# Attention with negated scores, first keys over two queues, and constants loaded as rows and turned by TensorE

## What is computed

```python
h = _norm(x) * (1 + scale1) + shift1           # shift, scale from silu(c) @ w_ada + b_ada
za, zb, q, k, v = split(h @ w_in)              # 512 | 256 | 512 | 512 | 512 columns
# A: gelu(za) -> u, v; v normed, mixed over 128 positions by a_ws, + a_bs; u * v
# B: 2-D DFT of zb, times f_w
# C, latent queries: 8 heads x 64, window of 8 x 16 keys + 512 cached context keys
s_loc = where(mask, q @ k.T * scale + rpb, -inf); s_ctx = q @ kc.T * scale
p = softmax(concat([s_loc, s_ctx]));              o = p_loc @ v + p_ctx @ vc
y = concat([A, B, C]) @ w_out; x = LN(alpha * x + gate1 * y); then a gated ConvFFN
```

## Time and profile before

| | |
|---|---|
| median of 3 runs | 2999.77 us (2996.41 to 3000.17) |
| the profiled execution, its own time | 3001.65 us |
| its span | 2999.9 us |
| PE busy | 2750.9 us (92%) |
| DVE, ACT, POOL busy | 1789.2, 1239.6, 472.0 us |
| mean granted clock of PE | 0.961 |

### The profile page before, as it was taken

One profiled execution on the slowest core, in us unless ns is written; L12 is line 12 of the kernel. 1 busy time (PEld: TensorE's weight loads), 2 busy tenths in 40 slices (PEclk: granted clock), 3 DMA queues, 4 the chain that ended last, 5 costly groups with the idle time before them and its releaser, 6 DMA issues. The chain is left out here.

```text
span 2999.9 us, 49988 instructions
## 1 busy us (share of the span) xinstructions
PE 2750.9 (92%) x17010; PEld 2484.5 (83%) x17010; DVE 1789.2 (60%) x3028; ACT 1239.6 (41%) x2612; POOL 472.0 (16%) x678
## 2 busy tenths in 40 slices
PE   4899999766999996997899999999999979999996
PEld 3899999655777785886899999999999968888875
DVE  3533432155999893776887876667666634452545
ACT  2111111124888882233655565556555522111121
POOL 0000000043444331224000000100000000320312
PEclk8999999878999997998899999999999989999998
DMA  8223222398576543563655564444444344344234
GB/s 277 85 74 123 85 85 71 136 372 170 118 148 141 114 91 98 186 209 117 189 166 171 177 200 160 152 151 147 154 150 153 124 158 150 99 133 140 77 126 133
DMA packets 405309, 435.71 MB, mean 145 GB/s; under 512 B 127228, under 2 KB 298254, under 8 KB 402448
## 3 DMA queue, kind: packets, MB, share of 16 engines
q1 hardware_dynamic: 379664, 415.20, 46.3%
q10 hardware_dynamic: 23168, 10.38, 1.2%
q0 software_dynamic: 2304, 7.88, 0.7%
HBM read 311.18 MB, written 124.57 MB: 145 GB/s over the span
## 5 line engine op out<-in xcount | busy, mean ns | idle before, releaser
L2138 PE MATMUL fu_alpha<-fu_h,fu_w 128*128 128x384 f32 x3168 | 576.1, 336 | 17.7 <-DVE fu_h L2364 10.6
L2624 PE MATMUL fd_acc<-fd_w,fd_f 128*128 128x512 f32 x2376 | 546.8, 392 | 27.2 <-DVE fd_w L2652 17.6
L2138 PEld LDWEIGHTS fu_alpha<-fu_h,fu_w 128*128 128x128 f32 x3168 | 554.9, 189 | 20.3 <-issue 20.2
L2624 PEld LDWEIGHTS fd_acc<-fd_w,fd_f 128*128 128x128 f32 x2376 | 447.5, 189 | 126.5 <-issue 18.3
L2138 PE MATMUL fu_beta<-fu_h,fu_w 128*128 128x384 f32 x1584 | 287.2, 336 | 0.6 <-DVE fu_h L2364 0.6
L2138 PEld LDWEIGHTS fu_beta<-fu_h,fu_w 128*128 128x128 f32 x1584 | 277.1, 189 | 1.1 <-issue 1.1
L579 PE MATMUL pj_gps<-pj_ht,w_in 128*128 128x256 f32 x2160 | 270.4, 286 | 0.0
L579 PEld LDWEIGHTS pj_gps<-pj_ht,w_in 128*128 128x128 f32 x2160 | 265.1, 192 | 1.3
L2648 DVE TENSOR_TENSOR fd_f<-fd_f_stage,fd_f 128x512 fp32r<-128x512 f32 (+1 forms) x110 | 91.3, 832 | 285.1 <-ACT fd_f L2604 285.1
L2604 ACT CAST fd_f<-fd_f_stage 128x512 fp32r<-128x512 f32 (+1 forms) x110 | 63.4, 579 | 444.1 <-PE fd_acc L2624 403.1
L2338 DVE TENSOR_TENSOR fu_w<-up_w_stage,fu_w 128x512 fp32r<-128x512 f32 x264 | 181.7, 689 | 85.7 <-ACT fu_w L2202 82.7
(11 more groups left out here) (218 smaller groups left out, 4161.6 us busy)
## 6 DMA issues: line engine op xcount, KB each, us to landing
up_w_stage<-in_w_gu_dram SPq DMA_DIRECT2D x88, 512.0 KB, 4.2
fu_w_sums<-w_gu_sums SPq DMA_DIRECT2D x132, 256.0 KB, 3.2
fd_w_stage<-in_w_down_dram SPq DMA_DIRECT2D x54, 512.0 KB, 3.7
fd_f_stage<-f_t SPq DMA_DIRECT2D x88, 256.0 KB, 2.7
at_k<-k_t SPq DMA_DIRECT2D x28, 704.0 KB, 12.5
w_gu_sums<-fu_w_sums SPq DMA_DIRECT2D x66, 256.0 KB, 4.5
fo_w<-in_w_ada_dram SPq DMA_DIRECT2D x8, 2048.0 KB, 14.8
up_w_stage<-in_w_gu_dram SPq DMA_DIRECT2D x44, 256.0 KB, 4.5
```

The lines of the kernel that those rows point to most:

```text
L2138: mm = pe.matmul(out, w[x][:, j, k, :], b[y][:, j, k, :], start=opens and (k, x, y) == (0, HI, HI), stop=(k, x, y) == (KH - 1, LO, HI), sk ...
L2624: mm = pe.matmul(acc[:, t, at], f[a][:, slot, t * P:(t + 1) * P], w[b][:, w_at(st, slot), at], start=is_step(st, 0) and (a, b) == (HI, HI) ...
```

## The change

The conditioning vectors, `b_ada` and `a_bs` arrive as 36 rows of 128 elements in an unused half of `zbt`; PE turns them in one transpose ahead of everything, ACT takes SiLU and DVE copies the rest from PSUM. `f_w` is issued after SiLU. In group 0 the rounding of weight blocks 4 to 8 is spread between the products on ACT and DVE, and `norm_x(2)` moves behind them (POOL follows). In attention `q` is stored with the factor negated, masks are +1e30, the bias is mask - rel, so that DVE seeks minima: the context minimum is the start value of the reduction over the window, which gives the bias of the exponentials (scale -1) itself. L1452 goes; a one-element copy that waits for the first reduction comes in. The sum of partial outputs is written at the head of the step instead of its end. The first keys and queries of head 0 go half over ACT's queue, ahead of ACT's other constants.

```diff
+        small = zbt[0:ROWS, 0, P:2 * P]
+        turned_small = abps[:, 0, 0:ROWS]
...
-    with nc.allow_non_contiguous_dma(reason="conditioning vectors, channel on partition"):
-        for v in (LAT, CTX):
-            sp.dma_start(cond[:, v, :], conds[v].rearrange("(k p) -> p k", p=P)).then_inc(cond_loaded, 16)
+    sp.dma_start(small[COND_ROW:BIAS_ROW, :], conds.rearrange("v (k p) -> (v k) p", p=P)).then_inc(small_loaded, 16)
...
-        if next2:
+        first_group = isinstance(g, int) and g == 0
+        if next2 and not first_group:
             row_rstd(g + 2)
         gate_rstd(g * NT + 1)
+        if first_group:
+            row_rstd(g + 2)
 
...
     act.dma_start(ident[:, :], ident_in).then_inc(consts_loaded, 16)
+    act.dma_start(small[BIAS_ROW:BS_ROW, :], b_ada[0, 0:2 * D].rearrange("(k p) -> k p", p=P)).then_inc(small_loaded, 16)
+    act.dma_start(small[BS_ROW:ROWS, :], a_bs.rearrange("l h p -> (l h) p")).then_inc(small_loaded, 16)
     act.dma_start(zbt[:, 0, 0:P], dft_c64).then_inc(consts_loaded, 16)
     act.dma_start(zbt[:, 1, 0:P], dft_s64).then_inc(consts_loaded, 16)
     act.dma_start(ws[:, :, :].rearrange("p a (b q) -> p (a b) q", q=P), a_ws.rearrange("l h p q -> p (l h) q")).then_inc(fw_loaded, 16)
+    act.wait_ge(silu_zeroed, 1)
+    act.wait_ge(small_turned, 1)
+    act.activation(silu[:, :, 0:2].rearrange("p k v -> p v k"),
+                   turned_small[:, COND_ROW:BIAS_ROW].rearrange("p (v k) -> p v k", v=2), ACT.Silu).then_inc(silu_done, 1)
     act.wait_ge(fw_zeroed, 1)
     for g in range(4):
...
-    act.wait_ge(cond_loaded, 32)
-    act.wait_ge(silu_zeroed, 1)
-    act.activation(silu[:, :, 0:2].rearrange("p k v -> p v k"), cond[:, :, :], ACT.Silu).then_inc(silu_done, 1)
-
-    with nc.allow_non_contiguous_dma(reason="biases, channel on partition"):
-        act.dma_start(mod_bias[:, :], b_ada[0, 0:2 * D].rearrange("(k p) -> p k", p=P)).then_inc(mod_bias_loaded, 16)
-        act.dma_start(bs[:, :], a_bs.rearrange("l h p -> p (l h)")).then_inc(consts_loaded, 16)
...
-    for n in range(3, len(W_BLOCKS)):
-        high_w(n)
+    high_w(3)
 
     def group(g, s, next2, next1, is_ctx):
-        if next1 is not None:
-            for j in range(SUB):
-                round_h(g + 1, 1 - s, j, used=g)
         unit, staged = [0], [0]
+        first_group = isinstance(g, int) and g == 0
+
+        def round_next():
+            if next1 is not None:
+                for j in range(SUB):
+                    round_h(g + 1, 1 - s, j, used=g)
+
+        def first_high(*blocks):
+            if first_group:
+                for n in blocks:
+                    high_w(n)
+
+        if not first_group:
+            round_next()
...
         gelu(0)
-        round_qk(HD ** -0.5)
+        first_high(4)
+        if first_group:
+            round_next()
+        round_qk(-(HD ** -0.5))
         n = product()
         act.wait_ge(ab_done, g * NT + NT)
         columns = gps[:, n, :].rearrange("p (m t q) -> p (m t) q", m=2, t=NT)
         if reversed_from(g, 0) is not None:
             columns = columns[:, :, P - 1::-1]
         act.copy(zbt[:, :, :].rearrange("p m (t q) -> p (m t) q", q=P), columns).then_inc(slot_read[n], 1)
+        first_high(5, 6)
         gelu(1)
-        round_qk(HD ** -0.5)
+        round_qk(-(HD ** -0.5))
+        first_high(7, 8)
         round_qk()
...
+    pe.wait_ge(consts_loaded, 16 * N_CONSTS)
+    pe.wait_ge(small_loaded, 48)
+    pe.transpose(turned_small, small[:, :], ident[0:ROWS, 0:ROWS]).then_inc(small_turned, 1)
...
+    dve.wait_ge(silu_done, 1)
+    dve.tensor_copy(mod_bias[:, :], turned_small[:, BIAS_ROW:BS_ROW]).then_inc(small_read, 1)
+    dve.tensor_copy(bs[:, :], turned_small[:, BS_ROW:ROWS]).then_inc(small_read, 1)
     norm_x(0)
-    dve.wait_ge(consts_loaded, 16 * N_CONSTS)
...
-    for n in range(2, 4):
+    for n in range(2, 5):
...
-        low_qk(0, 1, HD ** -0.5)
-        if isinstance(g, int) and g == 0:
-            for n in range(4, len(W_BLOCKS)):
-                low_w(n)
-        if next2:
+        first_group = isinstance(g, int) and g == 0
+
+        def first_low(*blocks):
+            if first_group:
+                for n in blocks:
+                    low_w(n)
+
+        low_qk(0, 1, -(HD ** -0.5))
+        first_low(5)
+        if next2 and not first_group:
             norm_x(g + 2)
         gate_norm(1)
-        low_qk(1, 4, HD ** -0.5)
+        first_low(6)
+        low_qk(1, 4, -(HD ** -0.5))
+        first_low(7, 8)
+        if first_group:
+            norm_x(g + 2)
...
-    load_qk(0, 0, first_loaded, (cols(4, 20), slice(T_ALL, KCOLS)), (cols(8, 16),))
+    load_qk(sp, 0, 0, first_loaded, first_k, first_q, (0,))
...
+    load_qk(act, 0, 0, first_loaded, first_k, first_q, (1,))
...
-            pool.tensor_tensor(from_cols, rel[:, parity, :, at],
-                               col_mask[:, c, 0:w].unsqueeze(1).to_broadcast([P, REL_TILE_ROWS, w]), ALU.add).then_inc(cols_done, 1)
+            pool.tensor_tensor(from_cols, col_mask[:, c, 0:w].unsqueeze(1).to_broadcast([P, REL_TILE_ROWS, w]),
+                               rel[:, parity, :, at], ALU.subtract).then_inc(cols_done, 1)
         pool.wait_ge(cols_done, h * 3 + c + 1)
         if not (isinstance(h, int) and h == 0):
-            pool.wait_ge(smax_done, (h - 1) * N_LAT + LAST_OF[i] + 1)
+            pool.wait_ge(nmax_done, (h - 1) * TILES + LAST_OF[i] + 1)
...
-    def row_max(tile):
+    def context_min(tile):
+
+        h, parity, pos = tile
+        s = pos % 2
+        n = blocks_of(pos)[0]
+        if n and pos == FIRST_OF[KIND_OF[pos]]:
+            dve.wait_ge(bias_ready, h * len(KINDS) + KIND_OF[pos] + 1)
+        dve.wait_ge(qk_done, h * TILES + pos + 3)
+        dve.tensor_reduce((cmin if n else nmx)[:, s:s + 1], ctx_ps[:, s, 0:T_PAST if n else T_CTX], AX_X,
+                          ALU.min).then_inc(cmin_done if n else nmax_done, 1)
+
+    def local_min(tile):
 
         h, parity, pos = tile
         s = pos % 2
         n = blocks_of(pos)[0] * blocks_of(pos)[1]
-        i = KIND_OF[pos] if n else None
-        if n and pos == FIRST_OF[i]:
-            dve.wait_ge(bias_ready, h * len(KINDS) + i + 1)
-        dve.wait_ge(qk_done, h * TILES + pos + 3)
-        dve.tensor_reduce(ncmax[:, s:s + 1], ctx_ps[:, s, 0:T_PAST if n else T_CTX], AX_X, ALU.max, negate=True).then_inc(cmax_done if n else nmax_done, 1)
         if n:
-            dve.tensor_tensor_reduce(prob[:, s, 0:n], loc_ps[:, s, 0:n], bias[:, BIAS_AT[i]:BIAS_AT[i + 1]], 1.0, 2 * MASKED,
-                                     ALU.add, ALU.max, lmax[:, s:s + 1]).then_inc(smax_done, 1)
-            dve.wait_ge(smax_done, h * N_LAT + pos + 1)
-            dve.scalar_tensor_tensor(nmx[:, s:s + 1], lmax[:, s:s + 1], -1.0, ncmax[:, s:s + 1],
-                                     ALU.mult, ALU.min).then_inc(nmax_done, 1)
+            i = KIND_OF[pos]
+            dve.wait_ge(cmin_done, h * N_LAT + pos + 1)
+            dve.tensor_copy(waited[:, :], cmin[:, s:s + 1])
+            dve.tensor_tensor_reduce(prob[:, s, 0:n], loc_ps[:, s, 0:n], bias[:, BIAS_AT[i]:BIAS_AT[i + 1]], 1.0, cmin[:, s:s + 1],
+                                     ALU.add, ALU.min, nmx[:, s:s + 1]).then_inc(nmax_done, 1)
 
...
-    def finish(tile):
+    def gather(tile):
         h, parity, pos = tile
         s = pos % 2
-        u = h * TILES + pos
-        dve.wait_ge(pv_done, u + 3)
+        dve.wait_ge(pv_done, h * TILES + pos + 3)
 
         dve.tensor_reduce(osum[:, s, :], o_ps[:, s, 0:3 * HD].rearrange("p (n d) -> p d n", n=3), AX_X, ALU.add).then_inc(o_read, 1)
 
+    def two_before(tile):
+        h, parity, pos = tile
+        if pos >= 2:
+            return h, parity, pos - 2
+        return None if isinstance(h, int) and h == 0 else (h - 1, 1 - parity, TILES - 2 + pos)
+
     def step(before, tile, after):
+        if two_before(tile) is not None:
+            gather(two_before(tile))
         if after is not None:
-            row_max(after)
+            context_min(after)
+            local_min(after)
         low_part(tile)
-        if before is not None:
-            finish(before)
         h, parity, pos = tile
         if pos == TILES - 1:
             dve.wait_ge(wo.w_hi, h + 1)
             dve.tensor_tensor(wo.w[LO][:, h, :], wst[:, parity, :], wo.w[HI][:, h, :].bitcast(F32),
                               ALU.subtract).then_inc(wo.w_lo, 1)
 
-    row_max((0, 0, 0))
+    context_min((0, 0, 0))
+    local_min((0, 0, 0))
     every_tile(dve, step)
+    gather((HEADS - 1, 1, TILES - 2))
     dve.wait_ge(out_done, HEADS * TILES - 2)
-    finish((HEADS - 1, 1, TILES - 1))
+    gather((HEADS - 1, 1, TILES - 1))
...
-            act.activation(prob[:, s, 0:n], prob[:, s, 0:n], ACT.Exp, bias=nmax,
+            act.activation(prob[:, s, 0:n], prob[:, s, 0:n], ACT.Exp, bias=nmax, scale=-1.0,
                            accum_out=sums[:, pos % 3, 0:1]).then_inc(exp_local_done, 1)
```

53 lines of the change are left out of this document (27 added, 26 removed).

## The result

The changed kernel takes 2967.88 us, the median of 4 runs (2966.37 to 2969.74), the kernel before in the same comparison 2999.97 (2996.41 to 3001.9): 32.1 us less, ratio 0.9895 with a 95% interval of 0.9878 to 0.9912. The forecast was 2970.5 (29.3 less), the range 2957 to 2985.

A forecast was written before the change was run, and what follows sets the result against it. PE is busy 92% of the span, so only its stands or lower-clock stretches can give time. Group 0 13.3, constants 2 and attention 14 sum to 29.3 us off 2999.8: 2970.5 us, range 2957 to 2985.

The forecast's parts named there:

- Group 0, 13.3 forecast: Projection's group 0: spreading the weight blocks removes stands of PE and cold-clock time, 13.3 us less, ends 8 and 17.
- 1.1 + 9.5 + 1.4 + 1.3: Group 0: first stand shrinks 1.1 us, stand before the mix goes 9.5, cold mix 1.4, cold product behind it 1.3.
- Rival 2: Group 0 finds a new wait and gives half of the 13.3 us: 2977 us; chance 0.12.
- Constants as rows, 2 forecast: Start, bound by transfers: small constants loaded as 36 rows give 2 us, between 0 and 4.
- what `pj_bs` delays: Start: the slow `pj_bs` load holds up the turning of `a_ws`, claimed to be over before the tokens come.
- 0.8 + 0.6 + 0.5: Start: 0.8 us from two slow transfer stretches, 0.6 from loads ahead of chunk 0, 0.5 from one SP issue less.
- L1452, 14 forecast: Attention: seven heads without waits for POOL give 16.4 us, net 14 after the copy's cost, ends -3 and 27.
- the 2 us for the copy: Attention: DVE pays about 0.07 us more per latent tile, 0 to 9 us in all, taken as 2.
- The copy's own wait: Attention: the one-element copy starts 0.27 us ahead of POOL's operation, so it was claimed not to wait.
- rival 1: Attention: the copy inherits the wait for POOL, so seven heads keep their waits: 2986.5 us; chance 0.12.
- Two queues, 0: Start of attention: first keys over two queues give 0 us, between -2 and +2; first scores stay near 701.5.
- Rival 4: Attention: DVE becomes the bound in all 128 latent tiles, at 0.30 us each, making the kernel slower, 3007 us; chance 0.04.

The follow-up runs named there:

- the order alone: Kernel before with only the new order of group 0 (weight blocks 4 to 8 spread between products, group 2's tokens normed last): 2986.52 us, 12.7 less.
- POOL's work cut: Kernel before with POOL's twelve larger bias operations of heads 1 to 7 cut to one element each, DVE's instructions all kept: 2983.57 us.
- the minimum apart again: Changed kernel with a one-element, two-operand minimum behind the window's reduction, which starts from a constant, and no copy: 2984.72 us.
- the minima alone: Kernel before with only attention's minima changes (negation, start value, copy, L1452 away, sum at the step's head), keys on SP's queue: 2984.08 us.
- the second copy: Changed kernel with another one-element copy behind the window's reduction, waiting for it, where L1452 stood: 2974.05 us, 6.2 slower than the changed kernel.

## Why the prediction was right

- **Group 0, 13.3 forecast, 13.6 measured.** Put on the old time scale (3.44 later), each step of the chain fell where it was put: modulation starts at 66.02 + 3.44 = 69.5 (forecast 69.4), the second pair is turned at 73.0 (73.0), the mix comes at 92.0 (92.4), blocks 7 and 8 are ready at 99.1 (98.8), `gate_norm` is in time by 2.9 (3). The terms: stands before ZB 3.82 down to 2.30, less 0.14 by which ZB ran longer, 1.38; then 9.50, 1.03 (mix) and 1.68 (the product behind it), against 1.1 + 9.5 + 1.4 + 1.3. The last term is the loosest: in other traces of the old order the product behind the mix took 6.60 and 6.75, which leaves 0.6 to 0.75, and the order alone gave 12.7 by the medians. The forecast had one stand before ZB; there were two, since the first pair of tokens also came 0.42 late. Rival 2 is out: DVE's blocks come before they are wanted.
- **Constants as rows, 2 forecast.** The trace has 3.4 in this pair and 2.8 over all fourteen traces, the medians of that part alone 1.7: inside my 0 to 4. I held that what `pj_bs` delays is over before the tokens come. The turn of `a_ws` stands ahead of the transposes that free the tokens' buffer, and SP issues the tokens of group 1 at 28.90 now and 37.13 before, so this needs a look. The bytes of the traces bear the argument out: the tokens are there when 14.9 to 15.1 MB have landed, in all fourteen traces, wherever between 28.8 and 37.1 us they were issued. What differs is when these bytes land. By 24 us, while the 4-byte elements pass, 6.9 to 7.1 MB have landed in the four traces with the old start and 7.9 in the ten with the new one (by 5 us already 0.23 against 0.73 MB in the first pair); between 24 and 40 us both land 5.9 to 6.0. The 0.95 MB of the first pair are 2.6 us at 370 GB/s. The forecast's sum had 0.8 + 0.6 + 0.5 for it.
- **L1452, 14 forecast, 16 measured.** The mechanism is shown three ways: POOL's work cut (-15.9, L1452 still there), the minimum apart again (+16.8, all else changed), the minima alone (-15.2). The Trainium skill (SBUF — State Buffer, Who interferes with whom) says that VectorE with two SBUF inputs and a GpSimd instruction that reads SBUF exclude each other. For POOL's large operations the traces agree, 50 of 51 such starts inside them were held; for its one-element operations they do not, none of 54 was. The mis-sized term is the 2 us for the copy: it and the reduction cost 0.14 a head by the kernel without POOL's work, 1.1 in all. Of the rest, head 0 gained 3.7 from the first value product to its cast, more than the 2.34 I gave each head, and the stretch from the last cast to the mix phase lost 1.5, of which 1.1 is the sum's new place, which I had put at 0.
- **The copy's own wait, free: right, for a reason I had only half.** I argued from the place, 0.27 us ahead of POOL. Place and form each suffice: at that place a two-operand form is caught 2 times in 128, and the copy is not caught at the worst place either. So rival 1 had no ground, for this copy. The same section of the Trainium skill also has the copy shut out where it runs in a two-port mode; no copy of one element here (71 that start inside POOL's operations in one trace) shows it.
- **Two queues, 0: right in sum, wrong in a step.** I let the first scores stay near 701.5; on that scale they came at 703.5, since the identity is now issued last and they wait for it. The product with values sets the end, and it moved by 0.4.
- **Rival 4's mechanism is real, its size was not.** The reduction with its start value in SBUF takes 0.06 us longer, as that rival feared, and the second copy shows that DVE ends last in a part of the tiles: 3.2 us more a head cost 0.8, a quarter. The change stayed below that because its copy (0.11 from the end of the context reduction to the next start, where the two overlapped by 0.09 before) and the 0.06 took the place of L1452's step, which I counted as 0.12 and which was 0.20. In the last head, from the end of the context reduction to the start of the low parts, DVE takes 0.58 us before, 0.64 now and 0.83 with the second copy. So my 0.07 a tile for DVE was near the 0.05 measured, but by two slips that cancel: the longer reduction left out, and L1452's step counted too short.

## What to carry to other kernels

A short instruction on VectorE that reads two operands in SBUF can cost several times its length where GpSimd works on large operands beside it; look at the longest beside the median of each small line, and take one operand away or move it, before anything is made shorter. When work is put into a gap of an in-order engine, ask which buffer it frees and who waits for that: a sum moved by one place cost 57 us. A stand of PE can be worth more than its length, where the product behind it runs at the lower clock: 2.3 us of stand gave 3.6 in the trace and 3.8 by the medians.

## What the runs showed of the hardware that was not expected

- A reduction over a window with a [128, 1] start value in SBUF takes 60 to 63 ns more than with a constant: 607 against 545 at 384 elements, 741 against 681 at 512.
- A copy of one fp32 element from SBUF to SBUF was never held by GpSimd, 0.152 to 0.156 us in 256 instructions of one trace, while the operation with two operands was held in 50 of the 51 cases in which it started inside POOL's bias operations (0.7 to 1.3 us), in each of two traces. Inside POOL's one-element operations it was held in none of 54.
- Traces of kernels with the same projection differ by 2 us at fourier's end (683.04, 680.95, 682.38), so steps below that are read from distances within one trace.
